# A mixer's rotary halves swapped by DMA across partitions instead of by a TensorE product

## The reference

```python
def apply_rope(t, cos, sin):
    t32 = t.astype(jnp.float32)
    half = HEAD_DIM // 2
    a, b = t32[..., :half], t32[..., half:]
    ...
    return jnp.concatenate([a * cs - b * sn, a * sn + b * cs], axis=-1).astype(t.dtype)

q_x, k_x, v_x, gu_x, gv_x = jnp.split(hx @ w_in, AB_SPLITS, axis=-1)
q_x = apply_rope(q_x.reshape(bsz, s_len, N_HEADS_A, 2, HEAD_DIM), cos, sin)
k_x = apply_rope(k_x.reshape(bsz, s_len, N_HEADS_A, 2, HEAD_DIM), cos, sin)
```

## Time and profile before

| What | Value |
|---|---|
| runs | 2031.79, 2033.56, 2035.4 us; median 2033.56 us |
| the profiled execution | 2028.85 us |
| its span | 2026.7 us |
| PE, DVE, ACT, POOL busy | 1725.1, 1468.2, 920.2, 624.9 us |
| granted TensorE clock, mean | 0.979 of full speed |
| rotary products (line 2220) | 16 records between 364.2 and 492 us |

### The profile page before, as it was taken

How to read it: one execution, slowest core, us unless ns; L and a number is a source line. 1 busy time by engine, 2 the same in 40 slices (tenths; PEclk the granted TensorE clock), 3 DMA queues, 4 the chain that set the end, 5 groups by cost and what they waited for, 6 DMA issues and landing times.

```text
span 2026.7 us, 22047 instructions
## 1 busy us (share of the span) xinstructions
PE 1725.1 (85%) x6989; PEld 1017.8 (50%) x6989; DVE 1468.2 (72%) x3271; ACT 920.2 (45%) x2398; POOL 624.9 (31%) x575
## 2 busy tenths in 40 slices
PE   4979998999896999987778778998999877778776
PEld 3759996988775544432233223454555322223222
DVE  7778888898876678666776776356877776777675
ACT  4664444445654445444444444334444444444443
POOL 1540000000004444343434443114445434443431
PEclk9989999999998999999999999999999999999999
DMA  9666677777749999999999999759999999999996
GB/s 384 264 228 229 249 281 271 270 251 249 268 162 359 420 421 421 421 420 418 422 421 421 422 421 421 265 203 409 419 417 420 421 421 422 421 421 421 421 422 255
DMA packets 119404, 723.25 MB, mean 357 GB/s; under 512 B 12012, under 2 KB 13828, under 8 KB 43000
## 3 DMA queue, kind: packets, MB, share of 16 engines
q0 software_dynamic: 75152, 541.35, 64.5%
q1 hardware_dynamic: 44136, 180.50, 24.2%
HBM read 720.72 MB, written 1.08 MB: 356 GB/s over the span
## 4 chain that ended last, share of the span: by engine, by line
DMA 39%; PE 30%; DVE 18%; ACT 5%; issue 4%; POOL 4%; SPq 0%; DVEq 0%; ACTq 0%; POOLq 0%
DMA X<-in_k_uv,EI 23%; PE PS L2321 12%; DMA Z<-in_k_uv,EI 10%; PE PS L2007 4%; DVE junk L1994 4%; PE PS L2009 3%; PE PS L2008 3%; PE PS L2297 3%; DMA W<-in_k_uv,EI 3%; DVE HALF L1614 2%; POOL X L1114 2%; DVE WL L1626 2%; DMA HALF<-in_k_ada 2%; DMA W<-in_k_ada 2%; PE PS L2338 1%
## 5 line engine op out<-in xcount | busy, mean ns | idle before, releaser
L2321 PE MATMUL PS<-X,dg 128*128 128x512 f32 x1380 | 663.6, 614 | 129.7 <-ACT dg L1123 127.0
L1994 DVE CUSTOM_DVE_ANT_0 junk<-H,X 128x1024 f32<-128x1024 f32 x345 | 422.0, 1223 | 236.9 <-DMA X<-in_k_uv,EI 222.1
L1114 POOL DMA_INDIRECT X<-in_k_uv,EI x345 | 369.4, 1071 | 509.2 <-PE PS L2321 361.4
L2321 PEld LDWEIGHTS PS<-X,dg 128*128 128x128 f32 x1380 | 248.4, 193 | 502.1 <-ACT dg L1123 281.6
L1123 ACT ACTIVATE CF<-DOT 128x1 f32<-128x1 f32 x512 | 103.6, 202 | 646.9 <-DVE DOT L1994 641.8
L2321 PE MATMUL PS<-Z,dg 128*128 128x512 f32 x480 | 233.7, 614 | 53.4 <-ACT dg L1123 53.0
L1123 ACT ACTIVATE dg<-CP,CG 128x128 f32<-128x128 f32 x512 | 205.6, 401 | 20.2 <-PE PS L2321 3.6
L1994 DVE CUSTOM_DVE_ANT_0 junk<-H,Z 128x1024 f32<-128x1024 f32 x120 | 146.9, 1224 | 88.4 <-DMA Z<-in_k_uv,EI 85.0
L2007 PE MATMUL PS<-XH,WH 128*128 128x256 f32 x592 | 172.3, 291 | 13.3 <-DVE WL L1626 12.0
L2321 PEld LDWEIGHTS PS<-Z,dg 128*128 128x128 f32 x480 | 84.1, 190 | 184.7 <-ACT dg L1123 117.3
L2008 PE MATMUL PS<-XL,WH 128*128 128x256 f32 x592 | 168.7, 285 | 0.0
(11 more groups left out here) (320 smaller groups left out, 2587.5 us busy)
## 6 DMA issues: line engine op xcount, KB each, us to landing
HALF<-in_k_ada SPq DMA_DIRECT2D x66, 512.0 KB, 5.4
W<-in_k_ada SPq DMA_DIRECT2D x24, 1024.0 KB, 7.1
Y<-in_k_ada SPq DMA_DIRECT2D x15, 1024.0 KB, 7.1
W<-in_k_win SPq DMA_DIRECT2D x15, 1024.0 KB, 7.5
W<-in_k_ffi SPq DMA_DIRECT2D x13, 1024.0 KB, 6.4
Y<-in_k_ffi SPq DMA_DIRECT2D x9, 1024.0 KB, 6.3
W<-in_ffn_w_out SPq DMA_DIRECT2D x8, 1024.0 KB, 5.0
W<-in_peer_wq SPq DMA_DIRECT2D x8, 1024.0 KB, 12.3
```

The source lines that it names most:

```text
L1114: e.indirect_dma_start(out=WS[k][:, :], out_offset=None, in_=I[f"k_uv{ly}"][:, :], in_offset=bass.IndirectOffsetOnAxis(ap=EI[t][:, j:j + 1 ...
L1994: e.tensor_tensor_reduce(junk, H[:, t, :], d[:, 0:D], 1.0, 0.0, ALU.mult, ALU.add, DOT[:, j:j + 1]).then_inc(v_dot, 1)
L2321: p = e.matmul(PS[:, 2 * t + q, :], dgb[n % 4][:, :], d[:, D + q * 512:D + (q + 1) * 512], start=(j == 0), stop=(j == 127))
```

## The change

The signs go into the sine table, so that the partner's value can be taken as it is. A new step `swap` stands directly behind the evacuation of a q or k tile: POOL waits for the evacuation and issues four DMAs from RO to Q2 or K2, each of 32 partitions of 512 values, which exchange the halves of 32 channels within each map. `rope2` then has a part on VectorE alone: it waits for the four DMAs (d_rope), multiplies dst by the sine in place and adds. It is put later in the list: of a q tile to the sixth quarter of its k tile (before: the third), and of a k tile to the third quarter of the following v tile (before: the sixth of its own). rotM leaves the constant tile CP, which shrinks from 912 to 784 columns.

```diff
-        group, rope, pend = 0, 0, None
+        group, rope, pend = 0, 0, []
...
-                if q in (2, 5) and pend is not None:
-                    P("rope2", *pend)
-                    pend = None
+                if pend and (tile, q) in ((pend[0][1] + 4, 5), (pend[0][1] + 4, 2)) and (q == 5 or pend[0][1] > 3):
+                    P("rope2", *pend.pop(0))
                 if q == 3:
                     P("evac", n, b, rope)
                     if tile < 8:
-                        pend = (rope, tile)
+                        P("swap", rope, tile)
+                        pend.append((rope, tile))
                         rope += 1
...
-        CP = at("CP", 40, [128, 912])
+        CP = at("CP", 40, [128, 784])
...
+        d_rope = [sem(f"d_rope{i}") for i in range(2)]
...
+        def rotary(tile):
+            return Q2[:, 2 * tile:2 * tile + 2, :] if tile < 4 else K2[:, 2 * tile - 8:2 * tile - 6, 256:512]
...
+                elif kind == "swap":
+                    i, tile = a
+                    dst, x = rotary(tile), RO[i % 2][:, :].rearrange("p (m n) -> p m n", m=2)
+                    w.wait_ge(a_ev, nth.ev[nth.rope_part[i]])
+                    for o in range(0, 128, 64):
+                        e.dma_start(dst[o:o + 32], x[o + 32:o + 64]).then_inc(d_rope[i % 2], 16)
+                        e.dma_start(dst[o + 32:o + 64], x[o:o + 32]).then_inc(d_rope[i % 2], 16)
...
-                    w.wait_ge(p_rope, i + 1)
+                    w.wait_ge(d_rope[i % 2], 64 * (i // 2 + 1))
                     e.tensor_tensor(x, x, cosT.unsqueeze(1).to_broadcast([128, 2, 256]), ALU.mult)
-                    e.tensor_tensor(dst, two(4), sinT.unsqueeze(1).to_broadcast([128, 2, 256]),
+                    e.tensor_tensor(dst, dst, sinT.unsqueeze(1).to_broadcast([128, 2, 256]),
                                     ALU.mult).then_inc(v_rp, 1)
...
-                elif kind == "rope2":
-                    i, b = a[0], 4
-                    w.wait_ge(a_ev, nth.ev[nth.rope_part[i]])
-                    take(b)
-                    e.matmul(PS[:, b, :], rotM, RO[i % 2][:, :], start=True, stop=True).then_inc(p_rope, 1)
-                    free[b] = [(v_rp, i + 1)]
...
-    cp[:, 384:640] = np.sin(ang)[:, i % 32].T
-    for o in range(128):
...
+    cp[:, 384:640] = np.where(i % 64 < 32, -np.sin(ang)[:, i % 32], np.sin(ang)[:, i % 32]).T
```

More of the change, by code:

```diff
@@ L738, in build @@
         R = [at(f"R{i}", 16 + 4 * i, [128, D]) for i in range(6)]
-        CP = at("CP", 40, [128, 912])
+        CP = at("CP", 40, [128, 784])
         ident, cosT, sinT = CP[:, 0:128], CP[:, 128:384], CP[:, 384:640]
-        rotM, iota, flip = CP[:, 640:768], CP[:, 768:784], CP[:, 784:912]
+        iota, flip = CP[:, 640:656], CP[:, 656:784]
         CB = [at("CB0", 44, [128, D])[:, :], at("CB1", 48, [128, D])[:, :], at("CB2", 190, [128, D])[:, :]]
@@ L852, in build @@
         g_init, g_an, g_gn8, g_own, g_fold = (sem("g_" + n) for n in ("init", "an", "gn8", "own", "fold"))
-        (p_small, p_xt, p_bias, p_part, p_y, p_as, p_at, p_ao, p_row, p_rope, p_ds, p_dt, p_do, p_gate, p_tt,
+        (p_small, p_xt, p_bias, p_part, p_y, p_as, p_at, p_ao, p_row, p_ds, p_dt, p_do, p_gate, p_tt,
          p_pq, p_rt, p_dg, p_pi, p_band, p_grp, p_po, p_w) = (sem("p_" + n) for n in (
-             "small", "xt", "bias", "part", "y", "as", "at", "ao", "row", "rope", "ds", "dt", "do", "gate",
+             "small", "xt", "bias", "part", "y", "as", "at", "ao", "row", "ds", "dt", "do", "gate",
              "tt", "pq", "rt", "dg", "pi", "band", "grp", "po", "w"))
@@ L1724, in _ @@
                     n = nth.rope_part[i]
-                    dst = Q2[:, 2 * tile:2 * tile + 2, :] if tile < 4 else K2[:, 2 * tile - 8:2 * tile - 6, 256:512]
+                    dst = rotary(tile)
                     x = RO[i % 2][:, :].rearrange("p (m n) -> p m n", m=2)
-                    w.wait_ge(p_rope, i + 1)
+                    w.wait_ge(d_rope[i % 2], 64 * (i // 2 + 1))
                     e.tensor_tensor(x, x, cosT.unsqueeze(1).to_broadcast([128, 2, 256]), ALU.mult)
-                    e.tensor_tensor(dst, two(4), sinT.unsqueeze(1).to_broadcast([128, 2, 256]),
+                    e.tensor_tensor(dst, dst, sinT.unsqueeze(1).to_broadcast([128, 2, 256]),
                                     ALU.mult).then_inc(v_rp, 1)
@@ L2388, in constants @@
     f = np.float32
-    cp = np.zeros((128, 912), f)
+    cp = np.zeros((128, 784), f)
     cp[:, 0:128] = np.eye(128)
@@ L2395, in constants @@
     cp[:, 128:384] = np.cos(ang)[:, i % 32].T
-    cp[:, 384:640] = np.sin(ang)[:, i % 32].T
-    for o in range(128):
[L2398 to L2403, removed]
+    cp[:, 384:640] = np.where(i % 64 < 32, -np.sin(ang)[:, i % 32], np.sin(ang)[:, i % 32]).T
+    cp[:, 640:656] = np.arange(16)
+    cp[:, 656:784] = np.eye(128)[::-1]
     tab = np.zeros((32, 1024), f)
```

## The result

The changed kernel took a median of 2036.28 us (20 runs, 2029.59 to 2039.94) beside 2032.65 us for the kernel before on the same chip: 1.0020 times as long, with an interval of 1.0014 to 1.0026. It is slower by 2.9 to 5.3 us. The forecast said 2.2 us faster: the sign is wrong. That the time lies in the forecast's range is luck: its upper end stood for six paid swaps less a gain of 1.72 us, and that gain didn't come.

The account below looks back on a forecast made before the run. The chain decides: TensorE up to 385 us, then VectorE's own work, broken by HALF weight loads. Terms -1.72 - 0.97 + 0.5 = -2.2 us from a median of 2033.56 gave 2031.4 us, range 2026.5 to 2036.5.

Parts of the forecast that it names:

- six paid swaps: Upper end of the range, 2036.5 us: six of the eight tiles' copies delay waited-for loads, -1.72 + 4.5 us.
- The products that go: Eight rotM products leave TensorE; the two on the chain before 385 us save 0.86 us each, together 1.72 us.
- that VectorE can follow: Supports the 1.72 us: from 366.48 to 372.64 VectorE is 1.93 us earlier, and the load landing at 385.05 moves up.
- the other six: Remaining rotary products on TensorE, 5.2 us, counted as nothing because VectorE sets the time there.
- The combinations that move: VectorE's rotary combinations go later; the second q/k pair's falls into load waits, gaining 0.97 us, bounds 0 and 1.93.
- The copies that come: 32 added DMAs, 0.75 us per tile, cost only where a waited-for HALF load overlaps: 0.5 us, bounds 0 to 6.0.
- The rule of the Trainium skill: Counterargument on DMA: all issuing engines share 16 queues; at 435 GB/s eight swaps cost 4.8 us, total 2.1 us slower.
- The copies delay HALF loads on VectorE's loop: Rival: copies hold up modulation-weight loads VectorE waits for; all eight paid gives 4.3 us slower, 2037.8 us; chance 0.08.
- three paid swaps and the 0.97 lost: Point where the sign turns: three tiles' copies cost 2.25 us against 1.72 gained, with the moved combinations' gain lost.
- The copies come late: Rival: a tile's four copies run one after another, 14.2 us past product 0's cover, giving 2045.6 us; chance 0.05.
- TensorE sets more of the time: Rival: later q/k pairs' removed products also gain; two pairs give 7.1 us, 2026.5 us; one gives 2028.2; chance 0.25.
- the HALF median above 6: Sign the forecast is wrong: modulation-weight loads taking over 6 us in the median from issue to landing.

Follow-up runs that it names:

- Two swaps only: Changed kernel with only the second q/k pair's two tiles copied, the other six tiles' exchange left out; 1.0013 times the kernel before.
- the second pair's late place alone: Kernel before, TensorE's products kept, only the second q/k pair's product and combination moved to the change's later place, no copies; 1.0000 times the kernel before.
- all late places: Kernel before with its eight TensorE products and combinations moved to the change's later places, no copies; 0.9997 times the kernel before.
- second dose: Changed kernel with every swap issued a second time, 32 more DMAs into the gate tile; 1.0048 times the kernel before.
- without products: Kernel before with TensorE's eight rotary products left out, combinations at their old places, no copies; 0.9997 times the kernel before.

## Why the prediction was wrong, step by step

**"The products that go", -1.72 us: failed, it was not gained.** In the changed kernel row maximum 0 comes 36.7 us after the start, before 36.4, both at the upper clock. Its chain in that profile no longer runs through TensorE's line up to there but through VectorE's, with a HALF load issued at 383.75 us that VectorE waits 2.04 us for. "Two swaps only" has no copy before this mark and the same clock, and is no earlier (37.0). So the copies didn't eat the gain. The step that failed is "that VectorE can follow": it argued that the last load before 385.05 would move up as well, but the waits for HALF, 0.46 and 2.22 us before, are 0.58 and 2.04. At the upper clock the loads stood only 0.5 us behind TensorE's line, so twice 0.86 us could not be gained there. Only where the clock had made TensorE late are the two products worth the 1.7 us. That the other six were worth nothing is borne out: TensorE now stands idle instead, 4.9 us between 386 and 443, where it had 0.2.

**"The combinations that move", -0.97 us: right as to size when alone, wrong as a term to be added.** From maximum 0 to 15 the second pair's late place alone gave -1.5 us, between the bounds 0 and 1.93, and all late places -2.7; the times can't tell either from nothing. But the prediction counted them and the copies separately. Together they cost 5.6 us of stretch. These two terms together said -2.7 us; the changed kernel without copies, in which they are all that is left of the change, measured -0.2 us by the times, within -2.0 and +1.6.

**"The copies that come", +0.5 us within 0 to 6.0: the term that was mis-sized, and the one that turned the sign.** It measured 4.2 us of stretch against the same kernel without copies, that is 5.6 of the eight swaps at the 0.75 us estimated from the earlier trace rows. The price for a paid swap may have been about right on average (the second dose, if all of it was paid, cost 0.78 each). What failed is how many are paid. The reason for the low end, "the loads waited for at 420.96 and 424.68 are issued between two swaps", looked at the loads that were late in the kernel before. The loads that became late are others, issued from 400 to 405 us, next to the K swap of the second pair. The DMA share of 0.76 was read as room, but it is a mean: from 405 to 410 us, with W, K swap and HALF loads together, there was none (1.01).

**The rule of the Trainium skill** cited there ("DMA: Bandwidth & Descriptors", Issuing engines are not separate DMA queues), that all transfers interleave on the same engines, gave, with that page's ceiling, 2.1 us slower if all swaps are paid. Its 4.8 us for the copies is close to the 4.2 measured, and the second dose, 0.78 us a swap where the ceiling gives 0.6, doesn't speak against it; its sum is nearer only because the -2.7 beside it were not gained. The row that the prediction put beside the rule, 512 KB behind 3 MB, is no support for it: POOL issued both, so it shows one engine's loads behind each other and not those of two.

**Rivals.** "The copies delay HALF loads on VectorE's loop" is what happened in kind, at a chance of 0.08 (which was for more than 4.1 us; the measured 2.9 to 5.3 lies across that mark). Its +4.3 is near the measured time partly by luck: it was the sum of 6.0 for the copies and -1.72 for the products, and these were 4.2 and nothing. Its condition, three paid swaps and the 0.97 lost, was set too far away because the 1.72 was taken as safe. "The copies come late" is out: they land 4.3 and 7.0 us after their issue, no combination waits. "TensorE sets more of the time" is out for the later pairs: without products it takes the same 170.1 us from maximum 0 to 15. (The six swaps that lead to the range's end make 2036.3 by the prediction's own sum, not 2036.5.) Of the signs named, the HALF median above 6 didn't come (5.1): a few loads at one place changed, not the median.

## What to carry to other kernels

A chain of waits names the path that ended last, not how far the next one stands behind it; before a piece on it is counted as gain, look for the second path at the same place, here a load that lands at the same mark, or leave the piece out and measure, with executions whose granted clock is the same at that place. A mean DMA share below 1 is no room for a copy: list what else is issued within the same few us, and do so with the order that the change makes, since a consumer that comes sooner also asks for its next load sooner. Where two edits act on the same ring of buffers, their effects aren't a sum, and only the kernel with both, and each alone, shows it.

## What the runs showed of the hardware that was not expected

GpSimd at work slows VectorE. In the kernel with GpSimd's sine products, POOL and VectorE in order of time:

```profile
365.67 2.17 POOL L1099 TENSOR_TENSOR Q<-RO,CP 32x512 f32<-32x512 f32 x1
```

```profile
362.14 1.22 DVE L1630 CUSTOM_DVE_ANT_0 HALF<-HALF,CB 128x1024 f32<-128x1024 f32 x1
...
364.39 2.31 DVE L1630 CUSTOM_DVE_ANT_0 HALF<-HALF,CB 128x1024 f32<-128x1024 f32 x1
```

The same instruction took 1.22 us before GpSimd had begun (at 364.05) and 2.31 beside it, and GpSimd itself took 1.3 to 2.3 us for one instruction on 32 partitions. The Trainium skill ("SBUF — State Buffer", SBUF: two separate sides) has the two engines share a pair of ports that one of them holds for a whole instruction while the other is fully blocked; the trace agrees in that VectorE's reads of two SBUF tiles grew (1473 and 1563 ns for 1220) and the one from PSUM didn't (1218). And ScalarE's copies of 512 columns took no less time for fewer partitions: 630 ns for 32 of them, 590 for an evacuation of 128.
